# A two-block hybrid transformer kernel: expert weights of the first block read eight rows to a partition, modulation weights in wider pieces

## What is computed

```python
mod = (c_act @ w_mod + b_mod).reshape(B_, 6, 1, D)          # w_mod: 1024 x 6144
...
h2 = rms_norm(x, g2) * (1 + mod[:, 4]) + mod[:, 3]
...
# hier_moe(h2): 32 experts in 4 groups, the 2 best of the best group for each token
logit_g = (h @ w_rg + b_rg).astype(F32)
logit_e = (h @ w_re + b_re).astype(F32)
...
def expert_block(args):
    xb, e = args
    g, u = jnp.split(xb @ w_up[e], 2, axis=-1)              # w_up[e]: 1024 x 1024
    return (jax.nn.silu(g) * u) @ w_down[e]                 # w_down[e]: 512 x 1024
```

## Time and profile before

| | us |
|---|---|
| median of 3 runs (lowest to highest) | 1628.95 (1625.55 to 1629.85) |
| the profiled execution | 1627.51 |
| its span, first to last instruction | 1625.6 |
| mean granted TensorE clock | 0.928 of full speed |
| HBM read | 477.05 MB |

### The profile page before, as it was taken

How to read it: one execution, slowest core, us unless ns; L and a number is a source line. 1 busy time by engine, 2 the same in 40 slices (tenths; PEclk the granted TensorE clock), 3 DMA queues, 4 the chain that set the end, 5 groups by cost and what they waited for, 6 DMA issues and landing times.

```text
span 1625.6 us, 31652 instructions
## 1 busy us (share of the span) xinstructions
PE 1325.0 (82%) x12376; PEld 694.1 (43%) x12377; DVE 441.5 (27%) x1329; ACT 394.2 (24%) x766; POOL 44.7 (3%) x68
## 2 busy tenths in 40 slices
PE   4999976878666776799969979987889897999875
PEld 3655443444332332355546544433337544444331
DVE  1004366432111121122234532211122533212112
ACT  2101234112111121122223312222232322222212
POOL 2100210000000000000000000000000000000000
PEclk9999988979998898899979988999899997999998
DMA  9969200769999999989764086999992145679994
GB/s 353 363 219 294 91 5 14 285 267 410 410 410 410 410 410 410 410 355 410 304 247 156 1 337 264 418 417 417 419 369 85 71 165 227 245 293 418 418 417 183
DMA packets 126304, 479.77 MB, mean 295 GB/s; under 512 B 9185, under 2 KB 19774, under 8 KB 109550
## 3 DMA queue, kind: packets, MB, share of 16 engines
q1 hardware_dynamic: 122496, 468.61, 73.6%
q0 software_dynamic: 2848, 8.86, 1.8%
q10 hardware_dynamic: 910, 1.59, 0.3%
HBM read 477.05 MB, written 1.97 MB: 295 GB/s over the span
## 4 chain that ended last, share of the span: by engine, by line
PE 58%; SPq 18%; DMA 10%; DVE 6%; issue 4%; ACT 2%; ACTq 0%; POOL 0%; DVEq 0%; PEldq 0%
SPq L511 18%; PE psum L1105 7%; DMA store<-in_w_up 7%; PE psum L1807 6%; PE psum L757 5%; PE psum L1083 5%; PE psum L1056 5%; PE psum L1096 4%; PE psum L1116 3%; PE psum L1803 2%; PE psum L1123 2%; PE psum L1345 2%; PE psum L1357 2%; PE psum L1390 1%; PE psum L634 1%
## 5 line engine op out<-in xcount | busy, mean ns | idle before, releaser
L1096 PE MATMUL psum<-store 128*32 128x256 f32 x2624 | 177.8, 412 | 64.8 <-DMA store<-in_w_expert_up 64.7
L1105 PE MATMUL psum<-store 128*32 128x256 f32 x2432 | 151.4, 405 | 30.9 <-DMA store<-in_w_up 30.4
L1247 DVE TENSOR_TENSOR store<-store,psum 128x128 f32<-128x128 f32 x79 | 22.7, 288 | 537.8 <-ACT store L1180 537.8
L1096 PEld LDWEIGHTS psum<-store 128*32 128x32 f32 x2624 | 79.5, 116 | 147.5 <-DMA store<-in_w_expert_up 95.2
L1056 PE MATMUL psum<-xn,store 128*32 128x256 f32 (+1 forms) x992 | 133.8, 501 | 3.7 <-DVE store L1210 3.7
L1083 PE MATMUL psum<-store 32*128 32x256 f32 (+1 forms) x992 | 128.1, 472 | 1.9 <-ACT store L1185 1.9
L1105 PEld LDWEIGHTS psum<-store 128*32 128x32 f32 x2432 | 85.6, 116 | 86.7 <-issue 37.8
L1180 ACT ACT_TABLE_LOAD x79 | 101.4, 1283 | 48.8 <-issue 48.5
L1180 ACT ACTIVATE store<-psum 128x128 f32<-128x128 f32 x79 | 21.9, 278 | 319.1 <-PE psum L1096 186.7
L1807 PE MATMUL psum<-store 128*128 128x512 f32 x224 | 97.7, 593 | 0.0
L1083 PEld LDWEIGHTS psum<-store 32*128 32x128 f32 (+1 forms) x992 | 58.2, 187 | 75.5 <-issue 70.2
(11 more groups left out here) (325 smaller groups left out, 1419.1 us busy)
## 6 DMA issues: line engine op xcount, KB each, us to landing
store<-in_w_expert_up SPq DMA_DIRECT2D x128, 1024.0 KB, 18.3
store<-in_w_expert_down SPq DMA_DIRECT2D x64, 1024.0 KB, 18.3
store<-in_w_gate SPq DMA_DIRECT2D x64, 1024.0 KB, 20.5
store<-in_w_up SPq DMA_DIRECT2D x64, 1024.0 KB, 22.1
store<-in_w_down SPq DMA_DIRECT2D x64, 1024.0 KB, 20.8
store<-in_w_mod SPq DMA_DIRECT2D x12, 2048.0 KB, 15.2
store<-in_w_in SPq DMA_DIRECT2D x6, 2048.0 KB, 12.9
store<-in_w_out SPq DMA_DIRECT2D x6, 2048.0 KB, 15.1
```

What stands on the lines that cost most here:

```text
L1096: mm = pe.matmul(out_(j), chosen_rows(k, 0), wt[:, kk, :, j, :], start=(k == 0), stop=(k == KD - 1))
L1105: mm = pe.matmul(out_(j), chosen_rows(k, e), wt, start=(k == 0), stop=(k == KD - 1))
```

## The change

- An expert's `w_up` and `w_down` of the first block are read with row 8p + k (4p + k for down) in partition p: two rows, 8 KB, contiguous in HBM and in the slot. A piece then spans all of the matrix, with 32 KB (16 KB for down) from one partition's run to the next.
- So that hidden feature 4n + j stands where the down pieces now need it, column group j takes every fourth column: the moving operand of L1096 has a step of four words.
- The token features must be in the same order: the norm uses `by_partition`, the router's weights are read `(p k) n`, and scale, shift and `norm2_g` are needed in an order by partition. POOL writes two more vectors of the modulation to HBM, word by word, and reads them back (`rows_pk`); ACT's queue gets one more parameter load; DVE waits for `rows_pk` before it forms the scale.
- A `w_mod` piece is half of the rows (four chunks) by 1024 columns, runs of 4 KB. Two pieces make one pair of sums; both `mod_mm` signals come in the second of them.

```diff
@@ first_sources, start_piece
-                src = ins["w_mod"][0].rearrange("(k p) n -> p k n", p=P)[:, :, 512 * j:512 * j + 512]
-                sp.dma_start(w_cols(slot, 512), src).then_inc(sem, 16)
+                half, pair = j % 2, j // 2
+                src = ins["w_mod"][0].rearrange("(k p) n -> p k n", p=P)[:, 4 * half:4 * half + 4, D * pair:D * pair + D]
+                sp.dma_start(piece_at(slot, 4 * D).rearrange("p (k n) -> p k n", k=4), src).then_inc(sem, 16)
...
-            up = ins["w_expert_up"][0].rearrange("e (k p) n -> e p k n", p=P)
-            down = ins["w_expert_down"][0].rearrange("e (k p) n -> e p k n", p=P)
+            up = ins["w_expert_up"][0].rearrange("e (p k) n -> e p k n", p=P)
+            down = ins["w_expert_down"][0].rearrange("e (p k) n -> e p k n", p=P)
@@ experts_pe, up
-                        wt = slot_ready(turn, i, piece).rearrange("p (k u q n) -> p k u q n", k=2, u=2, q=4)
+                        wt = slot_ready(turn, i, piece).rearrange("p (k u n q) -> p k u n q", k=2, u=2, q=4)
...
-                                mm = pe.matmul(out_(j), chosen_rows(k, 0), wt[:, kk, :, j, :],
+                                mm = pe.matmul(out_(j), chosen_rows(k, 0), wt[:, kk, :, :, j],
@@ POOL
-            for dram, part in zip(gates_dram, (2, 5)):
+            for dram, part in zip(gates_dram, (2, 5, 4, 3)):
...
-            pool.wait_ge(sems["gate_row"], 32)
+            pool.wait_ge(sems["gate_row"], 64)
+            for dram, dst in zip(gates_dram[2:], (scale_pk, shift_pk[:, :, 0])):
+                pool.dma_start(dst, dram.rearrange("(p k) -> p k", p=P)).then_inc(sems["rows_pk"], 16)
...
-            pool.dma_start(router_w[:, :, 0:NG], ins["w_router_group"][0].rearrange("(k p) n -> p k n", p=P))\
+            pool.dma_start(router_w[:, :, 0:NG], ins["w_router_group"][0].rearrange("(p k) n -> p k n", p=P))\
@@ TensorE, modulate_mm
-                w = w_cols(slot, 512)
-                for k in range(KD):
-                    for g in range(4):
-                        mm = pe.matmul(ps[j % 2][32 * g:32 * g + 32, 0:P], cT[:, k, :], w[:, k, P * g:P * g + P],
-                                       start=(k == 0), stop=(k == KD - 1))
-                mm.then_inc(sems["mod_mm"], 1)
+                w = piece_at(slot, 4 * D).rearrange("p (k n) -> p k n", k=4)
+                for n in range(2):
+                    for k in range(4):
+                        for g in range(4):
+                            mm = pe.matmul(ps[n][32 * g:32 * g + 32, 0:P], cT[:, 4 * half + k, :],
+                                           w[:, k, 512 * n + P * g:512 * n + P * g + P],
+                                           start=(half == 0 and k == 0), stop=(half == 1 and k == 3))
+                    if half == 1:
+                        mm.then_inc(sems["mod_mm"], 1)
@@ ACT's queue
+            act.dma_start(norm2_pk, ins["norm2_g"].rearrange("l (p k) -> p (l k)", k=KD)).then_inc(sems["params"], 16)
@@ DVE
-            link(dve.tensor_scalar(scaleT[:, 2, :], modT[:, 4 * KD:5 * KD, 0], 1.0, None, ALU.add))
-            link(dve.tensor_tensor(scaleT[:, 2, :], scaleT[:, 2, :], PT["norm2_g"], ALU.mult))
+            dve.wait_ge(sems["rows_pk"], 32)
+            link(dve.tensor_scalar(scale_pk, scale_pk, 1.0, None, ALU.add))
+            link(dve.tensor_tensor(scale_pk, scale_pk, norm2_pk, ALU.mult))
...
-            norm_dve(dve, at, link, scaleT[:, 2, :], modT[:, 3 * KD:4 * KD, :])
+            norm_dve(dve, at, link, scale_pk, shift_pk, by_partition=True)
```

More of the change, by code:

```diff
@@ L164 @@
 score neg_max exps probs tr tr_sb pv pv_sb a_sq a_ss a_mean a_sqrt mixed
-gate_row gate_mix_in gate_moe_in out_mm resid
+gate_row rows_pk gate_mix_in gate_moe_in out_mm resid
 logits lg lg_exp route rank_mm
@@ L175 @@
         "q_norm_g_2": 4, "kv_norm_g_2": 2, "pool_scale_2": 4, "diff_sub_g": 1, "gla_b_decay": 2, "gla_norm_g": 1}
-PARAMS = 16 * (len(ROWS) + 3)
+PARAMS = 16 * (len(ROWS) + 4)
 PARAMS2 = 16 * 12
@@ L326, in hybrid_kernel @@
         gain_pk = cols[:, 64:80].rearrange("p (l k) -> p l k", k=KD)
+        norm2_pk, scale_pk, shift_pk = cols[:, 40:48], cols[:, 48:56], cols[:, 56:64].unsqueeze(2)
         psum = ctx.enter_context(nc.psum_tensor("psum", [P, 8, 512], F32))
@@ L418, in hybrid_kernel @@
         gate_sb = vbf[:, D:2 * D]
-        gates_dram = [bias_dram[GRID * 28 * P + D * i:GRID * 28 * P + D * i + D] for i in range(2)]
+        gates_dram = [bias_dram[GRID * 28 * P + D * i:GRID * 28 * P + D * i + D] for i in range(4)]
         res_tmp = arena[:, 18432:19456]
@@ L1694, in _ @@
             pool.wait_ge(*at("mixed"))
-            pool.dma_start(router_w[:, :, 0:NG], ins["w_router_group"][0].rearrange("(k p) n -> p k n", p=P))\
+            pool.dma_start(router_w[:, :, 0:NG], ins["w_router_group"][0].rearrange("(p k) n -> p k n", p=P))\
                 .then_inc(sems["router_w"], 16)
-            pool.dma_start(router_w[:, :, NG:], ins["w_router_expert"][0].rearrange("(k p) n -> p k n", p=P))\
+            pool.dma_start(router_w[:, :, NG:], ins["w_router_expert"][0].rearrange("(p k) n -> p k n", p=P))\
                 .then_inc(sems["router_w"], 16)
@@ L1726, in modulate_mm @@
             def modulate_mm(j):
+                half = j % 2
                 slot = piece_ready(("mod", j))
-                w = w_cols(slot, 512)
-                for k in range(KD):
-                    for g in range(4):
-                        mm = pe.matmul(ps[j % 2][32 * g:32 * g + 32, 0:P], cT[:, k, :], w[:, k, P * g:P * g + P],
-                                       start=(k == 0), stop=(k == KD - 1))
-                mm.then_inc(sems["mod_mm"], 1)
+                w = piece_at(slot, 4 * D).rearrange("p (k n) -> p k n", k=4)
[7 more added lines that the diff above has]
+                        mm.then_inc(sems["mod_mm"], 1)
             def modulate_turn(j):
@@ L2028, in _ @@
             act.activation(oS, oS, ACT.Sqrt).then_inc(sems["a_sqrt"], 1)
-            norm_act(act, at, scaleT[:, 2, :], modT[:, 3 * KD:4 * KD, :])
+            norm_act(act, at, scale_pk, shift_pk)
             experts_act(act, at, 1, 0)
@@ L2273, in _ @@
             dve.wait_ge(*at("mixed"))
-            link(dve.tensor_scalar(scaleT[:, 2, :], modT[:, 4 * KD:5 * KD, 0], 1.0, None, ALU.add))
-            link(dve.tensor_tensor(scaleT[:, 2, :], scaleT[:, 2, :], PT["norm2_g"], ALU.mult))
+            dve.wait_ge(sems["rows_pk"], 32)
+            link(dve.tensor_scalar(scale_pk, scale_pk, 1.0, None, ALU.add))
+            link(dve.tensor_tensor(scale_pk, scale_pk, norm2_pk, ALU.mult))
             dve.wait_ge(sems["gate_mix_in"], 16)
             residual_dve(dve, at, link, 0, "out_mm", gate=gate_sb)
-            norm_dve(dve, at, link, scaleT[:, 2, :], modT[:, 3 * KD:4 * KD, :])
+            norm_dve(dve, at, link, scale_pk, shift_pk, by_partition=True)
             route_dve(dve, at, link, 1)
-            experts_dve(dve, at, link, 1, 0, scaleT[:, 2, :], modT[:, 3 * KD:4 * KD, 0])
+            experts_dve(dve, at, link, 1, 0, scale_pk, shift_pk[:, :, 0])
             dve.wait_ge(sems["gate_moe_in"], 16)
```

## The result

The changed kernel takes 1680.01 us (median; 1677.61 to 1681.52), the kernel before, run beside it, 1628.16 us (1625.55 to 1629.85). The ratio is 1.0319, 95% interval 1.0296 to 1.0343. The forecast of 1619.4 us and its range up to 1658 both missed it; the third case of rival A, a halved pace (1685 us), had a chance of 0.13 and is what came.

The account below looks back on a forecast made before the run. TensorE bounds the kernel except from 365.8 to 680.09 us, where SP's expert loads do. Terms -8.9 - 1.0 + 0.4 = -9.5 us give a median of 1619.4 us; range 1615 to 1658, leaving out the halved pace.

Parts of the forecast that it names:

- rival A: Up products (L1096): the stepped read is dear and the kernel ends slower; chances 0.12 (first two cases), 0.13 (halving), 0.02 (worse).
- a halved pace: Up products: reading one word from each place halves TensorE's pace, 3.59 us more a round, 1685 us in all; chance 0.13.
- Term 1: Expert loads of the first block in 8 KB runs go from 410 to 422 GB/s: -8.9 us, bounds 0 and 9.
- Rival B: Expert loads gain nothing from the new pitch, or runs stay at 4 KB: 1628 us, no change; chance 0.08.
- the sign in the chain: If the forecast is right, SP's expert loads (L511) stand in the chain for about 305 us.
- Term 2: Modulation pieces in 4 KB runs at 410 instead of 387 GB/s shorten the wait early in the kernel: -1.0 us.
- Term 3: One more parameter DMA on ACT's queue delays SP's pieces at the start: +0.4 us, bounds 0.2 and 1.
- Term 4: POOL's two extra scatters and two reads back (rows_pk) are all covered by waiting: 0.
- Term 5: Normalising with a step of eight words ends before TensorE has cleared its banks: 0; without that cover +0.8 us.
- Term 6: Up products reading every fourth word (L1096) cost 0; other end of the bound 2.1 us a round, ratio 1.58.
- The count of term 6: A step's price counts in 18.25 rounds: three before the loads set the pace, a quarter round, 15 after; 22 hide it.

Follow-up runs that it names:

- e1_contig: Changed kernel, but the up products read their 128 columns side by side again; loads stay as changed: 1627.38 us, ratio 0.9995.
- e4_before_step4: Kernel before with one edit, the up products read every fourth word: 1700.78 us, ratio 1.0445.
- e9_mod_only: Kernel before with only the modulation part of the change (w_mod in 4 KB runs, products regrouped): 1628.63 us, ratio 1.0001.
- e3_down4k: Changed kernel with down weights read by rows of 4 KB as before and no step in the up products: 1622.42 us, ratio 0.9964.
- e5_step3: Changed kernel with the first block's up products reading every third word: 1656.45 us in one run.
- e7_pairs: Changed kernel with the first block's up products reading pairs of neighbouring words, one pair in eight words: 1622.9 us in one run.

## Why the prediction was wrong, by its own steps

- **Term 1, the loads: right.** -8.9 us forecast at 422 GB/s; 421 to 422 came, and from the first round to the last landing 10.1 us are gone without the step (e1_contig) and 9.3 beside it (e4_before_step4 to the changed kernel). An estimate by the Trainium skill's "DMA: Bandwidth & Descriptors", section "Why small descriptors are slow (HBM only)", was 1.1%; the rate rose by 2.9% (410 to 422), so the measurement decides against that figure. Rival B falls. Only the sign in the chain, some 305 us of SP's loads, didn't come: up to 598.6 us the dearer rounds stand in their place.
- **Term 2, modulation: the wait as forecast, its worth at the end not shown.** The wait shrank by the forecast 1.0 us (0.8 in e9_mod_only), though the rate rose to 402 GB/s and not to the 410 of the sum; whether anything of it is left at the end lies below what these runs can tell.
- **Term 3, parameters: +0.4 forecast, 0 came** (12.89 us beside 13.12). **Term 4, POOL: 0, right.** The queue of the changed kernel in order of time:

```profile
145.57 3.59 POOL L1674 DMA_DIRECT2D bias_scratch<-small  x4 [93.87 <-DVE small L2071]
...
210.71 1.12 POOL L1694 DMA_DIRECT2D small<-bias_scratch  x2
...
247.17 0.54 POOL L1696 DMA_DIRECT2D store<-bias_scratch  x1 [35.34 <-DVE store L736]
```

The four scatters took 3.59 us of a queue that then still waited, and 35.34 us of waiting are left ahead of the gate's load. The two reads back were issued at 210.71 us, and DVE, which needs them at 295.40 (L2284), didn't wait. **Term 5, the norm: 0, right**, at 2.2 us; it ends at 320.0, while TensorE still clears its banks until the transposes of L854:

```profile
317.79 2.21 DVE L818 TENSOR_SCALAR xn<-X,small 128x1024 f32<-128x1024 f32 x2 [0.61 <-ACT small L802]
...
320.62 1.91 PE L854 MATMUL psum<-const_sb,xn 128*128 128x128 f32 x16
```

- **Term 6 failed: "I take 0" for the up products that read every fourth word.** It measured 3.8 us a round (7.4 against 3.59). The step that misled was to carry DVE's row over to TensorE: DVE at a step of eight words lost a factor of 1.58 against its fast form and nothing against its ordinary one, and from that I concluded that a word from a new place is delivered at the ordinary pace of any engine. The other end of the bound, 1.58, was too low as well: at the same step of eight words TensorE lost a factor of 2.09 (7.51 against 3.59 us). The slack that the term took for granted in TensorE's 0.88 ns a word isn't there: 3.77 us for a round at two words of a line is 1.84 ns a line and stream, 7.4 us at one word is 1.81 ns, so the pace without a step is close to what two words a line allow, and has no room for one.
- **The rival that named it.** The rule of the Trainium skill's "SBUF — State Buffer", section "Door 1: The DMA port swizzle", that full bandwidth wants two hits or more on a 16-byte line, pointed at the price, and all six orders of reading agree with it. The page gives no size; the halved pace was my reading of it, 1685 us, and 1680 came. The same passage goes on that for fp32 one can stride 4 for free. These runs say otherwise: a step of three words costs a factor of 1.57, of four 2.06. I had given the halved pace 0.13 because the single stepped row showed 1.58 and not 2.
- **The count of term 6 was too high.** It was 18.25 rounds; the 59.2 us of e4_before_step4 at 3.8 are 15.6. The 15.25 rounds from the last landing on paid nearly in full (56.2 us). The three rounds ahead of the paced stretch were to pay 3 x 3.8 = 11.4 us and the 22 paced ones nothing; together they cost 3.0. The first of them runs in part at half the clock, where the step costs little (last section). For the others the sign is in the loads: in 345 to 370 us they ran at 331 GB/s in the mean before, so they were not simply waiting for TensorE, and at 220 in e4_before_step4. The missing 2.8 MB are 6.8 us at 410 GB/s by estimate, 3.2 of them from the later start.
- **The sum** with what was measured: -9.3 to -10.1 (loads) + 3.0 + 56.2 = +49.1 to +49.9, and +2.6 for the later first round, so 51.7 to 52.5; the second block starts 52.4 us later, and the medians differ by 51.8. As the parts are cut from the same traces, this shows where the time lies and is no second proof; what is left for other mechanisms is below 1 us.

## What to carry to other kernels

Before a layout of longer runs is paid for by a step in TensorE's moving operand, count how many words of each 16 bytes the products use: with two or more the stream of 4-byte words here kept its pace within 7%, with one it took 2.0 to 2.1 times as long, alone or four abreast. Dealing the rows by twos made the kernel 8.2 us faster than before, and leaving the down weights in runs of 4 KB 6.1 us. A price that no row of a trace shows for an engine should not be bounded by another engine's row: where a stated rule gives a price beyond those bounds, it belongs inside the range.

## What the runs showed that was not expected

At half of the clock the step costs far less. The first up products of the block run at a granted clock of 0.50 for their first microseconds, and the 64 of them took 6.08 us before, 5.71 in e1_contig, 7.43 in the changed kernel and 7.44 in e4_before_step4: 1.4 to 1.7 us for the step where later rounds pay 3.8. The line of the up products in two microseconds at either clock, first before, then after (stretch, length, busy time and instructions of PE and of PEld, granted clock, DMA share, GB/s):

```profile
343.50:345.50 2.00, 2.00 (x24) 0.87 (x20) 0.50 0.00 0
697.00:699.00 2.00, 2.00 (x44) 1.19 (x39) 1.00 1.03 410
```

```profile
343.50:345.50 2.00, 2.00 (x20) 0.78 (x24) 0.50 0.01 4
697.00:699.00 2.00, 2.00 (x20) 0.59 (x16) 1.00 1.03 430
```

Without the step the number of instructions nearly doubles with the clock, 24 to 44 (those in flight at the edges are counted); with the step it is 20 at both, and the first round's 7.43 us are those of the later rounds. So the stepped stream didn't follow TensorE's clock here. At 1.2 GHz a round without the step would take 2 x 3.59 = 7.2 us by estimate, nearly the stepped 7.4, which leaves the step little to cost. Why the read has a pace of its own was not tested.

The start of that first round also scattered: 341.67 to 344.49 us over the changed kernel and its six variants that differ only behind it (e1_contig to e3_down4k, e5_step3 to e7_pairs), and 340.89 against 344.08 between the kernel before and e4_before_step4, which are the same up to there. A single profile alone can't book differences of 1 to 3 us there.
